# The ring slots of the split weights lie 32 bytes further apart than their size

## The reference

```python
for i in range(DEPTH):                       # DEPTH = 2
    h = rms_norm(x, mix_norm[i])
    y = mamba2_mixer(h, ...) if i == 0 else nsa_mixer(h, ...)
    x = x + y
    x = x + conv_ffn(rms_norm(x, ffn_norm[i]), ffn_w_gu[i], ..., ffn_w_down[i])
```

## Time and profile before

| | before |
|---|---|
| median of 3 runs | 2675.17 us (2671.46 to 2677.08) |
| the profiled execution: its time | 2680.16 us |
| its span, first to last instruction | 2678.5 us |
| PE busy, share of the span | 2639.5 us, 99% |
| DVE busy | 1788.2 us, 67% |
| ACT busy | 1430.1 us, 53% |
| mean granted clock of PE | 0.992 |

### The profile page before, as it was taken

One profiled execution on the slowest core, in us unless ns is written; L12 is line 12 of the kernel. 1 busy time (PEld: TensorE's weight loads), 2 busy tenths in 40 slices (PEclk: granted clock), 3 DMA queues, 4 the chain that ended last, 5 costly groups with the idle time before them and its releaser, 6 DMA issues. The chain is left out here.

```text
span 2678.5 us, 46463 instructions
## 1 busy us (share of the span) xinstructions
PE 2639.5 (99%) x15411; PEld 2322.0 (87%) x15411; DVE 1788.2 (67%) x2612; ACT 1430.1 (53%) x2210; POOL 196.9 (7%) x179
## 2 busy tenths in 40 slices
PE   7999999999999999999999999999999999999999
PEld 6888888888888888888888889888888888888888
DVE  7677777765677777775555766665677777775444
ACT  4676767654455555554444445654455555554443
POOL 0111111121200000000111000001300000000000
PEclk9999999999999999999999999998999999999999
DMA  5655555556555555556666556322555555556665
GB/s 183 217 192 193 191 192 183 193 171 188 177 188 188 188 188 188 187 187 184 190 188 189 178 191 193 99 94 77 183 184 188 187 188 188 187 188 186 187 187 168
DMA packets 135254, 481.94 MB, mean 180 GB/s; under 512 B 15104, under 2 KB 17152, under 8 KB 134160
## 3 DMA queue, kind: packets, MB, share of 16 engines
q1 hardware_dynamic: 132480, 467.72, 55.3%
q0 software_dynamic: 2336, 12.65, 1.4%
q10 hardware_dynamic: 368, 0.65, 0.1%
HBM read 478.80 MB, written 2.16 MB: 180 GB/s over the span
## 5 line engine op out<-in xcount | busy, mean ns | idle before, releaser
L965 DVE TENSOR_TENSOR w_lo<-raw,w_hi 128x1024 fp32r<-128x1024 f32 x900 | 1102.0, 1225 | 728.8 <-ACT w_hi L350 727.8
L350 ACT ACTIVATE w_hi<-raw 128x1024 fp32r<-128x1024 f32 x900 | 939.3, 1044 | 898.3 <-PE ps L683 878.4
L680 PE MATMUL ps<-xn,w_hi 128*128 128x512 f32 x4768 | 1208.4, 395 | 17.1 <-DVE xn L991 10.5
L680 PEld LDWEIGHTS ps<-xn,w_hi 128*128 128x128 f32 x4768 | 861.2, 189 | 179.9 <-DVE xn L991 11.1
L683 PEld LDWEIGHTS ps<-xn,w_lo 128*128 128x128 f32 x4768 | 651.8, 191 | 47.1
L683 PE MATMUL ps<-xn,w_lo 128*128 128x256 f32 x4768 | 665.7, 283 | 0.0
L680 PE MATMUL ps<-hid,w_hi 128*128 128x512 f32 x1408 | 355.6, 392 | 0.0
L680 PEld LDWEIGHTS ps<-hid,w_hi 128*128 128x128 f32 x1408 | 252.2, 189 | 44.4
L683 PEld LDWEIGHTS ps<-hid,w_lo 128*128 128x128 f32 x1408 | 194.2, 190 | 15.0
L683 PE MATMUL ps<-hid,w_lo 128*128 128x256 f32 x1408 | 198.8, 282 | 0.0
L359 ACT ACTIVATE cross<-ps 128x256 f32<-128x256 f32 (+1 forms) x366 | 132.7, 362 | 9.1 <-PE ps L683 9.1
(11 more groups left out here) (236 smaller groups left out, 1714.1 us busy)
## 6 DMA issues: line engine op xcount, KB each, us to landing
raw<-w_gu SPq DMA_DIRECT2D x352, 512.0 KB, 3.7
raw<-w_ssm_in SPq DMA_DIRECT2D x162, 512.0 KB, 3.6
raw<-w_down SPq DMA_DIRECT2D x128, 448.0 KB, 3.4
raw<-w_nsa_in SPq DMA_DIRECT2D x82, 512.0 KB, 3.6
raw<-w_ssm_out SPq DMA_DIRECT2D x64, 512.0 KB, 4.5
raw<-w_down SPq DMA_DIRECT2D x64, 512.0 KB, 3.6
raw<-w_nsa_out SPq DMA_DIRECT2D x32, 512.0 KB, 4.1
wcum<-cum_scratch POOLq DMA_DIRECT2D x8, 1024.0 KB, 7.4
```

Source lines behind the costliest of these rows:

```text
L350: act.activation(w_hi[:, slot, 0:n * P], raw[:, slot, 0:n * P], ACT.Copy).then_inc(unit_rounded, 1)
L680: pe.matmul(acc[:, 0:2 * n], w_hi[:, slot, cols], x[:, kb, 0:2 * n], start=(kb == 0), stop=False)
L965: TT(w_lo[:, slot, 0:n * P], raw[:, slot, 0:n * P], w_hi[:, slot, 0:n * P].bitcast(F32), ALU.subtract).then_inc(unit_split, 1)
```

## The change

The two rings of split weights get 8 more floats per slot, which nothing writes or reads. `raw` keeps its layout.

```diff
+SKEW = 8
...
         raw = sb("raw", [P, RING, UNIT * P])
-        w_hi = sb("w_hi", [P, RING, UNIT * P], F32R)
-        w_lo = sb("w_lo", [P, RING, UNIT * P], F32R)
+        w_hi = sb("w_hi", [P, RING, UNIT * P + SKEW], F32R)
+        w_lo = sb("w_lo", [P, RING, UNIT * P + SKEW], F32R)
         resid = sb("resid", [P, D_TILES, T])
         xn = sb("xn", [P, D_TILES, 2 * T], F32R)
```

## The result

The changed kernel takes 2687.0 us in the median of 5 runs (2683.59 to 2690.96), the one before 2672.6 (2671.18 to 2677.08). The ratio is 1.0051, 95% interval 1.0034 to 1.0067, which is 13.6 us (9 to 18); the medians alone differ by 14.4 us. The prediction was 2675 us, with 2664 to 2683 as its range and 0.10 for slower.

What follows compares the result with a forecast made beforehand. It took PE's matmul spacing, not waits, to bound the kernel. The profiled 2680.16 us plus 0 for each of three terms, restated for the runs' median 5.0 us lower, gave 2675 us, range 2664 to 2683.

Steps and rivals of the forecast that it cites:

- What bounds the kernel: PE never waits on split weights; its matmul spacing in one loop makes 2423 us, 90% of the span.
- Term (a): Whole kernel: the change adds no work, same instructions and same waits, 0 us.
- term (b): ACT's roundings and DVE's splits at other addresses: within 2% on DVE, covered by 5.9 us of slack, 0 us.
- Term (c): PE's reads of weights and activations: their distance does not change matmul spacing, taken as 0 us, extremes -53 and +27 us.
- the estimate by means: PE's matmul groups, priced by the mean of five compression-phase groups: -0.002 us a w_lo group, -5 us in all, taken as 0.
- three effects of addresses: The three rivals in PE's matmul spacing: small gain, chance 0.12; collision lifted, 0.02; slower, 0.10.
- The rival "slower": PE's loads of weights at odd multiples of 32 bytes, slots 1 and 3, take longer: +9 us, 2684 us, chance 0.10.
- The rival of a collision lifted: PE's matmul spacing holds a collision that the change lifts: 201 us less, 2474 us, chance 0.02.
- The small gain: The compression-phase mean hides a real effect of distance on both matmul halves: 2657 to 2670 us, put at 2665, chance 0.12.

Runs made afterwards that it cites:

- e1: Against the kernel before: a 32-byte pad ahead of raw moves every buffer by 32 bytes, no slot skewed; ratio 1.0004.
- e5: Against the kernel before: no skew, w_lo 480 bytes later and everything behind it 512 later, so w_lo's distance is 32 bytes in all slots; ratio 0.9962.
- e11: Against the kernel before: no skew, w_hi at a multiple of 256 bytes from the activations, w_lo at 16 bytes over one in all slots; ratio 0.9954.
- e12: Against the kernel before: no skew, w_hi at a multiple of 256 bytes, w_lo at 48 over one in all slots; 2650.79 us, ratio 0.9901.
- e8: Against the kernel before: a 96-byte pad behind raw moves all buffers but raw, so only distances to raw change; ratio 0.9995.
- e2: Against the kernel before: slots not skewed, w_lo 128 bytes later and all buffers behind it 256 bytes later; ratio 1.0035.
- e3: Against the kernel before: only the w_hi ring skewed by 32 bytes a slot, w_lo and later buffers 512 bytes later; ratio 1.0048.
- e4: Against the kernel before: only the w_lo ring skewed by 32 bytes a slot, later buffers 512 bytes later; ratio 0.9991.
- e9: Against the kernel before: w_hi skewed to distances 128, 96, 64 and 32 bytes in slots 0 to 3, w_lo at 32 in all; ratio 1.0028.
- e10: Against the kernel before: w_lo skewed by 16 bytes a slot to distances 64, 48, 32 and 16, w_hi at a multiple of 256; ratio 0.9956.
- e6: Against the kernel before: only the w_hi ring skewed, by 128 bytes a slot, w_lo and later buffers 512 bytes later; ratio 1.0011.
- e7: Against the kernel before: only the w_lo ring skewed, by 128 bytes a slot, w_hi at a multiple of 512 bytes; ratio 1.0010.

## Why the prediction was wrong

**What bounds the kernel** was right: PE, through the distance of its matmuls in one loop of 884 units, and no wait on a rounding or a split. **Term (a)**, no work added, and **term (b)**, 0 us for ACT and DVE, were right: the split is at 1245 ns as before, and no wait of PE names it.

**Term (c)** failed, at the sentence "the streams do not collide by their distance". It rested on the compression phase, where groups with a changing distance took 0.948 us in the mean against 0.95. Two things were wrong in that reading.

First, the reading was too coarse and too narrow. At 1 ns, eleven groups of 256 columns in that phase stand neither beside other work nor at the lower clock; they take 933 to 957 ns, 945 in the mean, against 952 in the gate/up phase. The five that were read, in steps of 10 ns, hid that. And a mean over all distances that equals the value at one distance does not show that the distance is without effect. For 256 columns the distance moves a group from 932 ns (32 bytes) to 962 (128), with 952 at 0; the mean over distances lies near the value before, and for `w_lo` the estimate by means held: -4 ns a unit in the changed kernel, where it gave -2.

Second, the 512-column matmul was given the price of the 256-column one, with the same sign and twice the size. That was the mis-sized term. Its group has 1841 ns at distance 0, the best of the eight multiples of 32 bytes; the seven others are at 1858 to 1875. The kernel before sat at that best point in all slots, and the skew took three of four slots off it, to 1862, 1873 and 1875. This is +19 ns a unit where I took 0 and allowed -40 to +20. I had written that no row showed a 512-column matmul at another distance; a term without any row, on 6944 matmuls, deserved more than the 0.24 that I gave to all three effects of addresses together.

**The rival "slower"** had the right side and nearly the right size (+9 us forecast, +13.6 measured), with the wrong mechanism: e1 puts every slot at an odd multiple of 32 bytes and costs nothing. Its sign in the profile, two slow `w_lo` groups out of four, did not come; three slow `w_hi` groups did. **The rival of a collision lifted** was right that the spacing holds something that depends on addresses, but the best choice that was tried gives 1% and not 7.5%. **The small gain** named a real effect with the wrong sign for this change; e5, e11 and e12 reach it and go past it. What I listed as the mark of an effect of the distance, groups that differ from slot to slot with the same four values again and again, is what the profile shows.

The Trainium skill, in "TensorE: Matmul & The Clock Gate", under "Step-by-step: what each phase is for", says that loading the next weights does not steal read bandwidth from the running matmul. The runs here show that the two are not independent at the level of 1 to 2% of a group: with e1, e8 and e5 together, the time follows the distance between the weights that are loaded and the activations that stream. Whether it is bandwidth that is lost, no run shows.

What stays open: the mechanism inside the memory. That two reads of PE meet is an inference from the distances and from the last `w_hi` matmul of e5. How a state is carried from one group to the next, and in e11 through a whole unit, was seen (e2, e3, e4, e9 to e12) but not explained. With the distance of a `w_hi` group at 0 it moves that group between 1826 (e12) and 1857 ns (e10), as much as the distance itself does. So no table of distances gives the best pair for both halves; sixteen steps of 16 bytes for each of two rings were tried in part only.

## What to carry to other kernels

When PE never waits, the addresses of the stationary and the moving operand are still worth 0.5% lost or 1% gained here: hold their distance modulo 256 bytes fixed over all buffers of a ring, and measure some distances for each width of matmul, one uniform shift a run, on the whole kernel, since the same distances cost 2773 ns a unit in one phase of e11 and 2803 in another. A skew between slots mixes several distances and gives something near their mean, so it can hide a good one; here the uniform 48 bytes for `w_lo` gave 0.990 and the 32-byte skew 1.005. And a mean over a quantity that agrees with one of its values is no proof that the quantity doesn't matter: ask for the spread, and for each form of instruction apart.

## What the runs showed of the hardware

- The spacing of fp32r matmuls with 128x128 weights depends on the distance between weights and activations in each partition, with a period of 256 bytes (e6, e7) and a resolution of 16 or finer (e5, e11 and e12): 932 to 963 ns for eight of 256 columns, 1826 to 1875 for eight of 512, at a granted clock of 1.00.
- It repeats within 1 ns in nine of ten repetitions of a slot in the second gate/up phase, and is blind to a common shift of all buffers by 32 bytes (e1) and to the distance to the buffer that ACT and DVE read (e8).
- A group depends on what ran before it as well: 1826 to 1857 ns for eight 512-column matmuls at distance 0 (e12, e10), and 933 or 954 for eight 256-column ones at 16 (e11).
